# Head norm by tile inside a recurrence's levels, sample attention between window tiles, and the first output rows begun early

## The chip, the cores and the metric

The kernel runs on one core of one Trainium2 chip. The metric is the time of one execution in microseconds (us); the median of three runs is compared. The engines run side by side, each through its own queue of instructions in the order in which they are written, and they wait for one another on semaphores: TensorE (PE; its weight loads are PEld), VectorE (DVE), ScalarE (ACT), GpSimd (POOL), and SyncE (SP), which issues the transfers.

## The reference, cut to what matters

One decoder layer in fp32 for 512 prompt tokens and 8 sample tokens (520 columns in all). The part around the change is the hybrid mixer: a delta-rule recurrence over 8 heads of 64, with a norm over each head, a bonus and an output gate, beside a sliding-window attention; both halves go through one output projection.

```python
S_final, y = lax.scan(step, wkv0.astype(F32), seq)            # 8 heads x 64, state 64 x 64
y = jnp.moveaxis(y, 0, 1)
mu = jnp.mean(y, axis=-1, keepdims=True)
var = jnp.mean(jnp.square(y - mu), axis=-1, keepdims=True)
yn = ((y - mu) * lax.rsqrt(var + GN_EPS)).reshape(B, T, C)
yn = yn * lp['ln_x_w'].astype(F32) + lp['ln_x_b'].astype(F32)
out = (yn + bonus.reshape(B, T, C)) * g                        # g = sigmoid(xg) @ w_g_up
...
o = jnp.einsum('bnkgqs,bnskd->bnqkgd', pr.astype(v.dtype), vc) # window of 128, softmax with sinks
...
y = jnp.concatenate([y_rwkv, y_swa.astype(y_rwkv.dtype)], axis=-1) @ lp['w_out']
```

Cross attention over 256 memory tokens and a mixture of experts (32, two chosen for each token) follow. Neither is touched.

## The kernel before

The prompt's 512 tokens are four tiles of 128; the 8 sample tokens are a fifth, small tile. Activations lie transposed in SBUF, channels on partitions: `yT` has eight chunks of 128 channels by 520 tokens, chunks 0 to 3 from the recurrence and 4 to 7 from the windows. After the input projection comes the stage that matters here. One list, `RECUR_ORDER`, sets the order of its steps, and every engine walks the same list and does its own share of each step. Its names: `AB`, `N0`, `level` (six per tile, each doubling an inverse by 64x64 products for two groups of four heads, `XM`, `MM`, `NN`) and `fin` (`akv`, `G`, `WT`) prepare a tile of the recurrence; `U`, `S` and `Y` apply it in two half tiles, and `Y` writes the tile's outputs to `yT`. `rq`, `rk`, `vk` rotate queries and keys. `ws` is a tile's window scores with the first half of its softmax: TensorE multiplies into four banks, VectorE scales, masks and takes the maxima (L1990, L1963 to L1967), ScalarE exponentiates (`exps`, L1665, L1667). `wp` is the other half: VectorE normalises (`normalise`, L1979 to L1981), TensorE transposes the probabilities (`pT`), ScalarE copies them, TensorE multiplies them with the values (`o`), ScalarE copies that to `yT`.

All eight PSUM banks go round in the order of `bank_plan()`. A product waits until the bank's tenant eight places earlier has been copied out (`reuse`), the copying engine waits until the product is done (`filled`), and `done` is a wait for a copy.

When the list has ended, the kernel before does the rest in a row: `wkvT` and `ysT` transpose the last state and the samples' outputs; `mean`, `gate` and `var` are eight products each of 128x128 by 260 columns (head sums by the matrix `bones` of ones, and the gate's projection) over all four channel chunks and both halves of the columns; then VectorE divides chunk by chunk (`deviation_divided`, L2100 to L2103, the reciprocal over 128x520) and applies the gate (L2122), which raises `s_fin`. Among this, the samples' own window attention runs (`kT`, `qd`, `ss`, `ssT`, a softmax of one row per head, `spT`, `so`). The output projection (`output_share`) takes for each tile of tokens and each half of 512 columns four products of the window chunks and four of the recurrence chunks (128x128 by 512). Three of the window parts, (0, 0), (0, 1) and (1, 0), are done while `s_fin` is still awaited; the rest follows it. SP reloads x and loads w_out's two halves (`wo`) at the end of the stage.

## Time and profile before

| | |
|---|---|
| median of three runs | 836.73 us (835.77 to 839.98) |
| profiled execution, its own time | 839.23 us |
| its span in the profile | 837.4 us |
| mean granted clock of TensorE, of full speed | 0.894 |
| PE busy | 702.7 us, 84% |
| DVE busy | 371.4 us, 44% |
| ACT busy | 214.9 us, 26% |
| recurrence, from the first level to the last `WT` copied | 222.6 to 346.0 us |
| rest of the windows, norm, gate, samples, until `so` is copied | 346.0 to 444.5 us |
| rest of the output projection and its norms | 444.5 to 502.9 us |

Busy time is work in flight on an engine; a granted clock of 1.00 is TensorE's 2.4 GHz and 0.50 its 1.2 GHz. Times in the text are microseconds from the start of the span. An fp32 product of the program is two MATMUL instructions in the trace, a transpose is one; the order view below counts a product once.

### The profile page before, as it was taken

How to read it: one execution, taken by the hardware profiler on the slowest of the kernel's cores; microseconds unless marked ns; L12 is line 12 of the kernel's file. 1: busy time of each engine (PE TensorE's matmuls, PEld its weight loads, DVE VectorE, ACT ScalarE, POOL GpSimd, SP SyncE). 2: the span in 40 equal slices, each digit the busy share in tenths (PEclk: the TensorE clock that was granted, in tenths of full speed). 3: DMA queues.
4: the chain of work that ended last, by engine and by line, in shares of the span. 5: the costliest groups of instructions: out<-in, count | busy, mean ns of one | idle time of the engine just before them, and what ended most of it. 6: DMA issues, size and time to landing. Idle time of an engine off the chain costs nothing.

```text
span 837.4 us, 16076 instructions
## 1 busy us (share of the span) xinstructions
PE 702.7 (84%) x6956; PEld 530.7 (63%) x6956; DVE 371.4 (44%) x740; ACT 214.9 (26%) x538; POOL 92.4 (11%) x122
## 2 busy tenths in 40 slices
PE   3999999999979898667997989877699269999933
PEld 3874887878878888556753448655246257777711
DVE  4210129993365575645483330354325742222216
ACT  4250115334222222434501110322112002222214
POOL 0100000000765000000000000000000024344210
PEclk9999999999999999957988998975789569999966
DMA  9622340002101000320407011023608849999725
GB/s 309 245 101 100 101 139 13 1 1 59 61 4 54 3 4 4 114 47 2 180 28 270 31 56 45 1 79 96 209 25 327 354 144 377 409 405 405 307 93 237
DMA packets 42492, 113.90 MB, mean 136 GB/s; under 512 B 10187, under 2 KB 12677, under 8 KB 41116
## 3 DMA queue, kind: packets, MB, share of 16 engines
q1 hardware_dynamic: 36964, 102.18, 33.2%
q0 software_dynamic: 4864, 8.53, 2.9%
q10 hardware_dynamic: 592, 2.13, 0.7%
q8 instruction: 56, 0.92, 0.4%
q14 instruction: 16, 0.13, 0.0%
HBM read 105.88 MB, written 16.24 MB: 146 GB/s over the span
## 4 chain that ended last, share of the span: by engine, by line
PE 70%; DVE 18%; ACT 5%; issue 4%; DMA 2%; SPq 0%; POOL 0%; POOLq 0%; DVEq 0%; ACTq 0%
PE bank L874 51%; PE bank L1494 7%; PE bank L878 5%; PE bank L1508 4%; PE bank L1480 2%; DVE arena L1918 1%; PE bank L1502 1%; ACT arena L1667 1%; DMA arena<-pair_d 1%; DVE arena L2100 1%; DVE arena L1963 1%; DVE arena L2032 1%; ACT arena L1684 1%; DVE arena L1990 1%; DMA arena<-hn_d,arena 1%
## 5 line engine op out<-in xcount | busy, mean ns | idle before, releaser
L874 PE MATMUL bank<-arena 64*64 64x64 f32 (+11 forms) x5156 | 527.4, 296 | 60.2 <-DMA arena<-pair_d 11.8
L874 PEld LDWEIGHTS bank<-arena 64*64 64x64 f32 (+5 forms) x5156 | 392.4, 158 | 183.9 <-issue 102.7
L878 PE MATMUL bank<-arena 128*128 128x128 f32 (+4 forms) x392 | 58.2, 301 | 50.9 <-issue 16.6
L878 PEld LDWEIGHTS bank<-arena 128*128 128x128 f32 (+4 forms) x392 | 50.3, 167 | 66.1 <-issue 27.9
L1494 PEld LDWEIGHTS bank<-arena 128*64 128x64 f32 x1024 | 58.6, 138 | 19.7 <-issue 19.7
L830 POOL DMA_INDIRECT arena<-hn_d,arena x16 | 16.7, 1044 | 434.3 <-DVE arena L2299 412.1
L1494 PE MATMUL bank<-arena 128*64 128x128 f32 x1024 | 63.5, 276 | 0.0
L2320 DVE TENSOR_TENSOR arena<-bank,arena 128x512 f32<-128x512 f32 x32 | 22.1, 692 | 54.5 <-PE bank L1480 54.5
L1599 ACT COPY arena<-bank 128x260 f32<-128x260 f32 x40 | 15.0, 375 | 108.1 <-PE bank L874 108.1
L834 POOL DMA_INDIRECT pair_d<-arena x32 | 31.8, 993 | 61.1 <-ACT arena L1801 54.1
L1699 ACT COPY arena<-bank 128x256 f32<-128x256 f32 x56 | 20.8, 372 | 63.8 <-PE bank L874 62.3
L2142 DVE TENSOR_TENSOR arena<-arena,bank 128x512 f32<-128x512 f32 x16 | 10.9, 684 | 57.4 <-PE bank L874 57.4
L1508 PE MATMUL bank<-arena 128*64 128x512 f32 x128 | 35.4, 632 | 0.9 <-ACT arena L1797 0.9
L1738 ACT ACTIVATE arena<-arena 128x1024 f32<-128x1024 f32 (+1 forms) x10 | 10.6, 1057 | 94.8 <-DVE arena L2142 86.6
L1874 DVE COPY arena<-arena 128x9 f32<-128x9 f32 x14 | 2.4, 171 | 67.5 <-ACT arena L1599 67.2
L1801 ACT COPY arena<-bank 128x512 f32<-128x512 f32 x32 | 18.7, 585 | 46.2 <-PE bank L1508 46.2
L1480 PE MATMUL bank<-arena 128*128 128x128 f32 x128 | 23.7, 312 | 7.6 <-DMA arena<-hn_d,arena 7.6
L787 POOL TENSOR_TENSOR arena<-arena 128x256 f32<-128x256 f32 x8 | 5.0, 620 | 183.8 <-PE bank L874 183.8
L2331 DVE TENSOR_TENSOR arena<-arena,bank 128x64 f32<-128x64 f32 x32 | 7.1, 221 | 40.6 <-ACT arena L1795 40.6
L1480 PEld LDWEIGHTS bank<-arena 128*128 128x128 f32 x128 | 17.4, 197 | 10.1 <-issue 7.4
L2054 DVE TENSOR_TENSOR arena<-arena,bank 128x256 f32<-128x256 f32 x40 | 16.3, 419 | 11.9 <-PE bank L874 11.2
L2169 DVE TENSOR_REDUCE arena<-bank 128x2 f32<-128x512 f32 x8 | 5.5, 688 | 33.9 <-PE bank L874 33.8
(238 smaller groups left out, 550.2 us busy)
## 6 DMA issues: line engine op xcount, KB each, us to landing
arena<-in_w_exp_gate SPq DMA_DIRECT2D x32, 512.0 KB, 10.9
arena<-in_w_exp_up SPq DMA_DIRECT2D x32, 512.0 KB, 13.2
arena<-in_w_exp_down SPq DMA_DIRECT2D x32, 512.0 KB, 14.2
arena<-in_w_in SPq DMA_DIRECT2D x5, 2048.0 KB, 9.5
arena<-in_x_prompt SPq DMA_DIRECT2D x8, 512.0 KB, 6.2
arena<-in_w_out SPq DMA_DIRECT2D x2, 2048.0 KB, 10.9
arena<-in_cache_mem_k SPq DMA_DIRECT2D x8, 512.0 KB, 7.5
arena<-in_cache_mem_v SPq DMA_DIRECT2D x8, 512.0 KB, 3.8
```

The lines of the kernel that those rows point to most:

```text
L830: pool.indirect_dma_start(dst, None, hn_d, bass.IndirectOffsetOnAxis(rows.bitcast(U32), 0), bounds_check=NT - 1, oob_is_err=False).then_in ...
L834: pool.indirect_dma_start(half_rows, bass.IndirectOffsetOnAxis(rows.bitcast(U32), 0), src, None, bounds_check=2 * PAIRS_E - 1, oob_is_err= ...
L874: last[0] = pe.matmul(out, lhsT, rhs, start=start, stop=stop, skip_group_check=True)
L878: last[0] = pe.transpose(out, in_, ident[0:n, 0:n])
L1480: ins = pe.transpose(bX[(2 * p + i) % 3][:, k * P:(k + 1) * P], xk[:, 4 * i + k, :], ident)
L1494: ins = pe.matmul(o[BS * g:BS * g + BS, 0:2 * BS].rearrange("p (a f) -> p a f", a=2), rows[:, k, :], w[:, 0:2, lo:lo + BS], start=k == 0, ...
L1508: ins = pe.matmul(bY[b % 2][BS * n:BS * n + BS, :], actT, wdn[b % NW][:, n * 512:(n + 1) * 512], start=True, stop=True, skip_group_check=True)
L1599: return act.copy(dst, o[:, 0:HALF])
L1699: act.copy(dst[(n + 1) % 2][:, 4 * q:4 * q + 4, :], o[:, 0:256].rearrange("p (h t) -> p h t", h=4)).then_inc(evac["a"], 1)
L1801: act.copy(yb[b % NB3], bY[b % 2][:, :]).then_inc(s_ay, 1)
L2054: tt(Xi[:, qs, :], Xi[:, qs, :], o[:, 0:256].rearrange("p (h t) -> p h t", h=4), ALU.add) \
L2320: tt(xTe[p % 2][:, 4 * i:4 * i + 4, :], bX[n % 3][:, :].rearrange("p (k n) -> p k n", k=4), g, ALU.mult) \
```

## The change

The work that stood behind the list becomes steps of the list. `gate` products stand between the levels of tile 0. `mean`, `sq`, `var` of tile t-1 stand in tile t's levels: four products of 128x128 by 128 columns for the means, a Square on ScalarE, and four products with the squares as the stationary operand and two columns as the moving one, which give a variance per token and head (128x8) where before it was spread over all channels (4 x 128x520). `rstd` takes the root on ScalarE and the reciprocal on VectorE of that small array, once for tiles 0 to 2 and once for tiles 3 and 4 (`GROUPS`). `rb` spreads it back over the channels by products with the identity, and `y_final` multiplies, adds the bonus and applies the gate, again once per group. `wp` is split into `wt` (normalise, transposes) and `wv` (values). The steps of the windows and of the samples come in another order, and `wo` projects tile 0's output rows (sixteen products) before the last window tile and the samples' attention are done. Loads of x for tiles 2 to 4 wait for the norm, since the gate now lies in their place.

The core of the diff:

```diff
+RECUR_ORDER = [("AB", 0, 0), ("AB", 0, 1), ("N0", 0, 0),
+               ("level", 0, 0), ("gate", 0, 0), ("level", 0, 1), ("gate", 0, 1),
...
+        RECUR_ORDER += [("level", _t, 2), ("rq", 2 * _t - 2, 0), ("mean", _t - 1, 0), ("level", _t, 3),
+                        ("rq", 2 * _t - 2, 1), ("sq", _t - 1, 0), ("level", _t, 4), ("rq", 2 * _t - 1, 0),
+                        ("level", _t, 5), ("var", _t - 1, 0), ("rq", 2 * _t - 1, 1)]
...
         RECUR_ORDER += [("rk", 0, 0), ("level", _t, 2), ("rk", 0, 1), ("rk", 1, 0), ("level", _t, 3), ("rk", 1, 1),
-                        ("vk", 0, 0), ("level", _t, 4), ("ws", 0, 0), ("level", _t, 5)]
+                        ("vk", 0, 0), ("mean", 2, 0), ("level", _t, 4), ("ws", 0, 0), ("sq", 2, 0), ("level", _t, 5),
+                        ("var", 2, 0)]
     RECUR_ORDER += [("fin", _t, 0)]
-RECUR_ORDER += [("ws", 1, 0), ("U", 3, 0), ("wp", 0, 0), ("S", 3, 0), ("ws", 2, 0), ("U", 3, 1), ("wp", 1, 0),
-                ("S", 3, 1), ("ws", 3, 0), ("Y", 3, 0), ("wp", 2, 0), ("wp", 3, 0)]
+RECUR_ORDER += [("rstd", 0, 0), ("U", 3, 0), ("wt", 0, 0), ("S", 3, 0), ("wv", 0, 0), ("U", 3, 1), ("ws", 1, 0),
+                ("Y", 3, 0), ("S", 3, 1), ("wkvT", 0, 0), ("ysT", 0, 0), ("ws", 2, 0), ("wt", 1, 0),
+                ("mean", 3, 0), ("mean", 4, 0), ("wv", 1, 0), ("ws", 3, 0), ("kT", 0, 0), ("sq", 3, 0), ("sq", 4, 0),
+                ("wt", 2, 0), ("var", 3, 0), ("var", 4, 0), ("ss", 0, 0), ("wv", 2, 0), ("rb", 0, 0), ("ssT", 0, 0),
+                ("rstd", 1, 0), ("wo", 0, 0), ("wt", 3, 0), ("wv", 3, 0), ("rb", 1, 0), ("spT", 0, 0), ("so", 0, 0)]
+GROUPS = ((0, 3), (3, 5))
...
+            def head_variances(t, _):
+                R = tile_rows(t)
+                pe.wait_ge(s_ysq, t + 1)
+                o = reuse(pe, ("var", t))
+                for c in range(4):
+                    src = ysq[:, c, :] if t < TILES else ysqS[:, c, :]
+                    mm(o[0:R, 2 * c:2 * c + 2], src, bones[:, 0:P:HD])
+                close()
+
+            def deviations_spread(g, _):
+                pe.wait_ge(s_rs, g + 1)
...
+                            for e in range(2):
+                                mm(o[64 * e:64 * e + 64, n:n + R],
+                                   rs[0:R, t, 2 * c + e:2 * c + e + 1].to_broadcast([R, HD]), ident[0:R, 0:R])
...
+            def first_rows_projected(t, _):
+                weights_in(pe, ("wo", 1))
+                done(pe, ("o", t))
+                for n in range(2):
+                    output_share(t, n, windows, True)
+                    if n == 0:
+                        weights_in(pe, ("wo", 0))
+                        pe.wait_ge(s_fin, 1)
+                    output_share(t, n, recurrence, False)
+                    close()
...
+                elif what == "sq":
+                    R = tile_rows(t)
+                    done(act, ("mean", t))
+                    act.activation(ysq if t < TILES else ysqS, yT[:, 0:4, t * P:t * P + R], ACT.Square) \
+                        .then_inc(s_ysq, 1)
...
+                elif what == "rstd":
+                    lo, hi = GROUPS[t]
+                    done(act, ("var", hi - 1))
+                    act.activation(rs[:, lo:hi, :], rs[:, lo:hi, :], ACT.Sqrt, scale=1.0 / HD,
+                                   bias=small[:, 40:41]).then_inc(s_dev, 1)
...
+            def y_final(g):
+                lo, hi = GROUPS[g][0] * P, min(GROUPS[g][1] * P, NT)
...
+                    ins = stt(yT[:, c, lo:hi], o[:, n:n + W], pcol("ln_x_w", c), yT[:, c, lo:hi], ALU.mult, ALU.mult)
...
+                    ins = stt(yT[:, c, lo:hi], yT[:, c, lo:hi], pcol("ln_x_b", c), PR[:, 8 + c, 1 + lo:1 + hi],
+                              ALU.add, ALU.add)
+                link(ins)
+                done(dve, ("gate", 3, 1))
+                tt(yT[:, 0:4, lo:hi], yT[:, 0:4, lo:hi], gateS[:, :, lo:hi], ALU.mult).then_inc(s_fin, 1)
...
-                link(dve.reciprocal(ydev[:, c, :], ydev[:, c, :]))
```

Where it moves instructions, first on TensorE at the end of tile 3's levels. In the program before: level 4 (32 products), the scores of window tile 0 (128x128 x8), then level 5, `akv`, `G` and `WT` (64x64 x64) in one run.

```order
L874 MATMUL bank<-arena 64x64 x32
L874 MATMUL bank<-arena 128x128 x8
L874 MATMUL bank<-arena 64x64 x64
L874 MATMUL bank<-arena 128x256 x8
L874 MATMUL bank<-arena 64x64 x8
L878 MATMUL bank<-arena 128x128 x8
L874 MATMUL bank<-arena 64x128 x8
```

In the changed program, at the same place: the mean of tile 2 (128x128 x4), level 4, the scores, level 5 (64x64 x16), the variances of tile 2 (128x2 x4), then `akv`, `G`, `WT` and the first `U` (56).

```order
L898 MATMUL bank<-arena 128x128 x4
L898 MATMUL bank<-arena 64x64 x32
L898 MATMUL bank<-arena 128x128 x8
L898 MATMUL bank<-arena 64x64 x16
L898 MATMUL bank<-arena 128x2 x4
L898 MATMUL bank<-arena 64x64 x56
L902 MATMUL bank<-arena 128x128 x8
```

Four variance products now stand ahead of `akv`, and the scores of window tile 1 (128x256 x8), which followed `WT`, have moved behind the transposes of tile 0 (L902).

ScalarE at the same place, changed program: the eight exponentials of window tile 0 (L1733), then tile 2's Square (L1788), the copy of its variances (L1793), `WT`'s copies (L1771), the root (L1797) with its table load, and the copies of tile 0's transposed probabilities (L1750).

```order
L1731 ACTIVATE arena<-arena 128x8
L1733 ACTIVATE arena<-arena 128x128 x8
L1788 ACTIVATE arena<-arena 128x512
L1793 COPY arena<-bank 128x8
L1771 COPY arena<-bank 128x4x64 x2
L1797 ACT_TABLE_LOAD
L1797 ACTIVATE arena<-arena 128x24
L1750 COPY arena<-bank 128x2x128 x4
```

The Square, its copy and the root stand between the exponentials and the copies; before, `WT`'s copies came straight after the exponentials.

VectorE towards the end, changed program: `y_final` of tiles 0 to 2 (L2078, L2083, L2087), the samples' scores and maxima (L2207 to L2043), the second reciprocal, the residual adds of tile 0 (L2223), and only then the normalisation of window tile 3 (L2055 to L2057) and `y_final` of tile 3 and the samples.

```order
L2078 SCALAR_TENSOR_TENSOR arena<-bank,arena 128x384 x4
L2083 SCALAR_TENSOR_TENSOR arena<-arena 128x384 x4
L2087 TENSOR_TENSOR arena<-arena 128x4x384
L2207 TENSOR_SCALAR arena<-bank 64x128
L2039 TENSOR_REDUCE arena<-arena 64x1
L2041 TENSOR_TENSOR arena<-arena 64x1
L2042 TENSOR_TENSOR arena<-arena 64x1
L2043 TENSOR_SCALAR arena<-arena 64x1
L2191 RECIPROCAL arena<-arena 128x16
L2223 TENSOR_TENSOR arena<-arena,bank 128x512 x2
L2055 TENSOR_TENSOR arena<-arena 128x8
L2056 RECIPROCAL arena<-arena 128x8
```

The normalisation of window tile 3 stood ahead of the whole norm before; now it stands behind the projection of the first rows.

## Rows read from the trace of the kernel before

**Rows 1.** The page: the span, and each engine's busy time, share and instructions.
```profile
span 837.4 us, 16076 instructions
...
PE 702.7 (84%) x6956; PEld 530.7 (63%) x6956; DVE 371.4 (44%) x740; ACT 214.9 (26%) x538; POOL 92.4 (11%) x122
```
**Rows 2.** Timeline of PE in the levels: start us, us, engine line, count, [idle before].
```profile
222.58 14.70 PE L874 MATMUL bank<-arena 64*64 64x64 f32 x480 [2.00 <-DVE arena L2038]
...
249.04 22.27 PE L874 MATMUL bank<-arena 64*64 64x64 f32 x618 [2.58 <-DVE arena L2038]
```
**Rows 3.** Busy time of DVE in a stretch of tile 1's levels 3 to 5.
```profile
262.30:272.40 10.10, 8.78 (x21) 1.00 0.27 108
```
**Rows 4.** Timeline of PE from tile 3's level 4 to the windows' end.
```profile
335.82 5.73 PE L874 MATMUL bank<-arena 64*64 64x64 f32 x144
343.28 5.12 PE L874 MATMUL bank<-arena 64*64 64x64 f32 x96 [1.73 <-DVE arena L2063]
354.45 1.94 PE L878 MATMUL bank<-arena 128*128 128x128 f32 x8 [6.04 <-issue]
357.09 10.50 PE L874 MATMUL bank<-arena 128*64 128x128 f32 x80 [0.70 <-ACT arena L1684]
374.19 3.65 PE L878 MATMUL bank<-arena 128*128 128x128 f32 x16 [6.60 <-issue]
378.52 10.52 PE L874 MATMUL bank<-arena 128*64 128x128 f32 x178 [0.68 <-ACT arena L1684]
...
397.24 2.04 PE L874 MATMUL bank<-arena 128*64 128x128 f32 x32 [0.68 <-ACT arena L1684]
```
**Rows 5.** Timeline of ACT: the last exponential of window tile 0, then `WT`'s copies.
```profile
345.25 0.19 ACT L1667 ACTIVATION_READ_ACCUMULATOR arena<-arena 128x1 f32 x1
345.34 0.62 ACT L1704 COPY arena<-bank 128x256 f32<-128x256 f32 x2
```
**Rows 6.** Timeline of DVE: window tile 2's last bank, its maxima, tile 1's normalisation.
```profile
366.58 0.69 DVE L1990 SCALAR_TENSOR_TENSOR arena<-bank,arena 128x512 f32<-128x512 f32 x1 [0.59 <-PE bank L874]
367.31 2.29 DVE L1963 TENSOR_REDUCE arena<-arena 128x8 f32<-128x2048 f32 x1
...
371.36 0.17 DVE L1979 TENSOR_TENSOR arena<-arena 128x8 f32<-128x8 f32 x1
371.56 0.20 DVE L1980 RECIPROCAL arena<-arena 128x8 f32<-128x8 f32 x1
371.80 2.29 DVE L1981 TENSOR_TENSOR arena<-arena 128x2048 f32<-128x2048 f32 x1
```
**Rows 7.** Clock by stretch: busy PE, PEld, DVE, ACT, POOL, then PEclk, DMA share, GB/s.
```profile
352.00:382.50 30.50, 20.07 (x142) 16.97 (x144) 11.88 (x20) 12.43 (x43) 0.00 (x0) 0.50 0.20 43
...
420.25:427.00 6.75, 6.75 (x19) 4.31 (x18) 5.98 (x7) 0.00 (x0) 0.00 (x0) 0.50 0.02 8
```
**Rows 8.** Timeline of PE from `mean` to the output projection.
```profile
405.23 11.26 PE L874 MATMUL bank<-arena 128*128 128x260 f32 x52 [0.28 <-DVE arena L2084]
...
418.31 10.24 PE L874 MATMUL bank<-arena 64*128 64x4 f32 x40 [0.95 <-ACT arena L1730]
...
436.55 3.69 PE L874 MATMUL bank<-arena 128*64 128x2 f32 x64 [0.32 <-DVE arena L2118]
444.58 18.87 PE L874 MATMUL bank<-arena 128*128 128x512 f32 x40 [4.34 <-DVE arena L2125]
...
464.18 13.90 PE L874 MATMUL bank<-arena 128*128 128x512 f32 x32
```
**Rows 9.** Groups of DVE from 395 to 500 us: count, busy us, mean ns.
```profile
L2100 DVE RECIPROCAL arena<-arena 128x520 f32<-128x520 f32 x4 | 13.6, 3396 | 2.0 <-ACT arena L1726 2.0
...
L2090 DVE SCALAR_TENSOR_TENSOR arena<-bank,arena 128x260 f32<-128x260 f32 x8 | 3.1, 422 | 0.8 <-PE bank L874 0.8
```
**Rows 10.** Timeline of ACT at the first root: table load and next instruction.
```profile
412.95 1.28 ACT L1726 ACT_TABLE_LOAD   x1
414.25 3.05 ACT L1726 ACTIVATE arena<-bank,arena 128x260 f32<-128x260 f32 x8
```

More of the change, by code:

```diff
@@ L671, in _, with load_projection @@
                     .then_inc(s_cache, 16)
+            def load_projection(i):
+                key, s, src, k = loads[i]
+                sp.dma_start(weights(key, k), src).then_inc(s_w[s], 16)
+            sp.wait_ge(full, place[("Y", 3, 1)] + 1)
+            load_projection(n_early + 1)
+            sp.dma_start(x[:, 0, :], A["x_prompt"][0, 0:P, :]).then_inc(s_xr[0], 16)
+            sp.dma_start(x[:, 1, :], A["x_prompt"][0, P:2 * P, :]).then_inc(s_xr[1], 16)
             done(sp, ("wkvT",))
@@ L1214, in window_outputs @@
                 close()
-            steps = {"rq": rotated_query, "rk": rotated_key, "vk": window_values, "ws": window_scores,
-                     "wp": window_outputs, "sample": lambda *_: None,
-                     "tok": by_token, "AB": chunk_products, "N0": first_N, "level": level, "fin": last_products,
-                     "U": updates, "S": state, "Y": outputs}
-            for what, t, n in RECUR_ORDER:
-                steps[what](t, n)
-            o = reuse(pe, ("wkvT",))
-            done(pe, ("S", 3, 1))
@@ new lines, in states_turned, with sample_outputs_turned @@
+            def states_turned(*_):
+                o = reuse(pe, ("wkvT",))
+                done(pe, ("S", 3, 1))
+                for c in range(4):
+                    tr(o[0:64, c * P:(c + 1) * P], ST[:, 8, c, :])
+                close()
+            def sample_outputs_turned(*_):
+                pe.wait_ge(s_ysl, 16)
+                o = reuse(pe, ("ysT",))
+                for c in range(4):
+                    tr(o[:, c * NS:(c + 1) * NS], ysr[:, c * P:(c + 1) * P])
+                close()
@@ L1313, in _ @@
+            for what, t, n in RECUR_ORDER:
+                steps[what](t, n)
+            done(pe, ("o", 3))
             done(pe, ("so",))
-            pe.wait_ge(s_fin, 1)
-            weights_in(pe, ("wo", 0))
+            pe.wait_ge(s_fin, 2)
             def rows_transposed(key, first, t):
@@ L2138, in residual @@
                     ins.then_inc(evac["v"], 1)
-                for n in range(2 if t < TILES else 0):
+                for n in range(2 if t < TILES and not begun else 0):
                     o = filled(dve, (key, t, n))
```

345 lines of the change are left out of this document (186 added, 159 removed).

## The prediction

> **What bounds the kernel now.** I read the page first, then the clock by stretch, then each engine's timeline between 220 and 503 us. TensorE is busy for 84% of the span [rows 1], so the first question for moved work is whether TensorE has room where it lands. In the levels of the recurrence it has none: tile 0's run of 480 instructions takes 14.70 us and tile 1's run of 618 takes 22.27 us without an idle gap inside [rows 2]. The reader is to see there that a product added between levels is paid in full. VectorE has 1.3 us free in 10.1 us of tile 1's levels 3 to 5 [rows 3], so it has no more room than TensorE at that place.
>
> After the levels, from 346 to 404 us, the stage is bound by the round trip of the window softmax, not by one engine. TensorE stands idle for 6.04 and 6.60 us ahead of the transposes at 354.45 and 374.19 [rows 4]. The trace puts these waits down to "issue"; the programs' order and rows 6 say what they are: after the last bank of window tile 2 (366.58) VectorE takes 0.69 us, then 2.29 us and the small steps for the maxima, and only then tile 1's normalisation (0.17, 0.20, 2.29 us), which ends at 374.09. The transposes start 0.1 us later. In this stretch the granted clock is 0.50, the lower level (1.2 GHz), from 352 to 382.5 us [rows 7]; it fell after an idle gap, so that the gap costs twice.
>
> From 415 to 444.5 us VectorE sets the end: four reciprocals over 128x520 take 13.6 us [rows 9], and TensorE waits for the last of that work for 4.34 us [rows 8]. This is the wait that the change removes.
>
> **The change part by part.** The profiled execution has a span of 837.4 us and a time of 839.23 us; the median of the runs is 836.73 us, 2.5 below it. I sum on the span and add the difference to the median.
>
> *Products from the tail into the levels.* The 26 products at 405.23 (8 means, 8 gates, 8 variances, 2 small) take 11.26 us [rows 8], 0.433 us each. Eight gates in tile 0 cost 8 x 0.433 = 3.5 us, since TensorE has no gap there [rows 2]. A mean of one tile is four products of 128 columns: 4 x 0.433 x 128/260 = 0.85 us. For a variance of two columns there is no such row: `so` has 64 instructions with two columns in 3.69 us [rows 8], 0.058 each, so eight instructions are 0.46 us; the weights here are twice as wide, so up to 0.9; I take 0.6. VectorE's subtraction of the mean (128x512, 0.69 us [rows 6]) fits beside the mean's product, the variance lies half under VectorE's backlog. I take 1.35 us for each of tiles 1 and 2 (bounds 0.85 and 2.1): 2.7 us. **Levels: +6.2.** From here on I keep the axis of the trace before and leave these 6.2 out.
>
> *The wait at tile 3.* Here the moved work does more than fill time. The variances of tile 2 need its Square, and the Square stands on ScalarE behind the eight exponentials of window tile 0 (both orders are shown above). Those end at 345.44 [rows 5]; with tile 2's mean (+0.85) at 346.25; a Square over 128x512 is about 0.6 us (ScalarE's two copies of 256 columns take 0.62 [rows 5]), so TensorE gets to the variances at 346.9. It has done level 5 by 341.5: level 4, scores, level 5 and `akv` are the 5.73 us from 335.82 [rows 4], less `akv`'s 0.9 (32 instructions at 14.70/480 [rows 2]), plus 0.85. It then stands for 5.4 us, and behind the wait are `akv`, `G` and `WT`, so also VectorE's copies and `U`. From the variances: 1.0, `akv` 1.9 (32 instructions at the lower level, which I expect after such a gap), copy 0.7, `G` 1.9, `WT` about 1.5, ScalarE's copies 0.62 [rows 5]: 353.5. Before, `WT` was copied at 345.96. **Wait: +7.5** (bounds 6.0 at full clock, and 9).
>
> *From `WT` to the samples' end.* The path before takes 345.96 to 444.53 us, 98.6. The new one, step by step. ScalarE loads a table (1.28 [rows 10]) and takes the root, VectorE inverts 128x24 and does `U`'s three small adds (1.2): 356.5. It normalises window tile 0, half as wide as tile 1, in about 1.6: 358.1. TensorE transposes (1.94) and then has the same 80 instructions as before at 357.09 (10.50 [rows 4]), with tile 1's scores in place of tile 2's: 370.6. `Y` and the second `S` are 130 instructions of the 178 that took 10.52; 6.2, so 376.8; the state's copy and two small transposes 1.2; the scores of tile 2 3.4 (eight products of 256 columns at 0.426): 381.4. Now the same round trip: last bank and maxima 3.6, normalisation 2.75 [rows 6]: 387.8, and TensorE has stood for 6.4 us. Transposes of tile 1 at the lower clock 3.65 [rows 4], means 1.25, values 2.04 [rows 4], scores of tile 3 3.4, `kT` 1.2: 399.4. Round trip again: 405.0, idle 5.6. Transposes 3.65, variances 1.4, `ss` 3.4 (32 of the 40 instructions at 418.31 [rows 8], most of them at 0.50 [rows 7]), values 2.7, `rb` of 48 instructions at 2.04/32 each 3.1 [rows 4]: 419.3. `y_final` on VectorE: at 0.42 for 260 columns [rows 9] and 0.69 for 512 [rows 6], 384 columns take 0.55; last bank 0.55, four adds 2.2, gate over 1536 columns 1.75 (2.29 for 2048): 423.9. The window half of the first rows (four products of 13.90/16 = 0.87 us [rows 8]) lies under that, the other twelve take 10.4: 434.4. Only then does VectorE reach tile 3's normalisation: add 0.7, 2.75: 437.8, idle 3.4. Transposes 2.4, values 2.4, `rb` 1.8, `y_final` of 136 columns behind it 2.2: 446.6. Samples' normalisation, transpose and copy 1.3, `so` 3.69 [rows 8] to 5 at the lower clock, copy 0.2: 452.3. That is 98.8 us from `WT`. **Tail: +0.2.** VectorE's 13.6 us of reciprocals and the 11.26 us of products are gone, but 13.9 us of projection and about 5 us of `rb` stand in their place, and the scores of each window tile come one round later.
>
> *The rest.* At 444.58 twenty products were left of the first two tiles, 18.87 us [rows 8]. Now sixteen are left: 13.9, and 1.0 for the lower clock after `so`. **Rest: -4.0.** What follows is the same program. w_out's and x's loads move, but they are issued over 15 us ahead of their use.
>
> Sum: 6.2 + 7.5 + 0.2 - 4.0 = 9.9 us, so a span of 847.3 and a median of 836.73 + 9.9 = 846.6 us.
>
> *What the skill says here.* Each switch of the root's and the exponential's tables costs 1.30 us in this trace, load and all: the load starts at 412.95 and the next instruction at 414.25 [rows 10]. The Trainium skill, ScalarE: Activation LUTs, What ACT_TABLE_LOAD costs, puts a switch at 1283 ns for the load and about 1380 ns more for a drain. By the page the first root would come 1.4 us later and the sum, as an estimate, would be 11.3. The trace has the load but no drain in front of the next instruction, so I stay with the row.
>
> **The rivals.**
>
> *The moved products are free.* If the levels have gaps which the timeline merges away, the 6.2 us of step one cost nothing: 840.4 us, no change that can be told. For it: TensorE's ends are modelled. Against it: tile 1's run is paced evenly and VectorE is as full [rows 2, 3].
>
> *The clock stays up.* The tail has more for TensorE between softmax rounds. If the granted clock were 1.00 from `WT` on, the same steps end earlier: `WT` at 352.0, window tile 1's scores at 363.8, tile 2's at 372.1, tile 1's normalisation at 378.4, tile 2's at 394.5, `rb` at 405.9, `y_final` at 410.4, first rows at 420.9, `so` at 438.0. That is 14.3 us less than 452.3: 9.9 - 14.3 = -4.4, a time of 832.3 us, faster. It decides between `WT` and the end of `Y`, where I have 17 us of half clock. Against it: before, the clock stayed at 0.50 from 352 to 382.5 us though TensorE was busy for 20.07 of 30.5 us [rows 7], and I count gaps of 5.4, 4, 6.4 and 5.6 us, as long as those that it fell in.
>
> *VectorE's end is all that counts.* One could take the 29 us from 415.1 to 444.5, put 9 us of `y_final` against 24 us of division and gate, and forecast 822 us. Against it: `y_final` waits for `rb`, and `rb` for window tile 2 ahead of it on TensorE, which the sum shows to be as late as before.
>
> *The lower clock also in the first rows.* Twelve more products at half speed and a slower `so` are up to 7 us: 854 us.
>
> **How the numbers follow.** The sum's own case, 842 to 853, has 0.58 (the wait's bounds, and 4 us either way for the clock of the tail). Free products: 0.17. Clock up: 0.15. VectorE alone: 0.03. Lower clock in the first rows: 0.07. About 0.5% (4.2 us) is what a measurement of this kernel can tell from no change. So faster 0.18, same 0.17, slower 0.65. The range goes from 834 to 854, which leaves out most of the clock's rival and the last one's end; the likeliest case's own range is 842 to 853. The time is the likeliest's, 846.6 us.
>
> **What would show it.** In the changed profile: TensorE's run in tile 0's levels is about 3.5 us longer; an idle gap of about 5 us ahead of the variances at tile 3, released by the Square on ScalarE; `WT` copied about 13.7 us later than before (7.5 + 6.2); three gaps of 5 to 6.5 us ahead of the windows' transposes, and one of about 3.4 us ahead of tile 3's; a clock of 0.50 through window tile 1's scores; `so` copied near 458 us; VectorE's busy time about 17 us lower. The prediction is wrong if the clock is 1.00 after `WT`, or if the Square does not come late; then the time falls towards 832 to 840.

## The result, and the profile after

The changed kernel takes 848.65 us (median of four runs, 846.91 to 858.77), the kernel before on the same chip 838.13 (four runs): ratio 1.014 [1.010, 1.0185]: slower by 1.4%, with an interval clear of 1. A second comparison gave 854.38 against 837.5, ratio 1.0215 [1.0176, 1.0253]. The profiled execution is the shortest of the first four: 846.91, with a span of 845.1 against 837.4 before. So the profiles differ by 7.7 us where the medians differ by 10.5; the terms below add up to the 7.7.

The page of the changed kernel, answering to [rows 1]:

```profile
span 845.1 us, 16345 instructions
...
PE 710.4 (84%) x7084; PEld 539.8 (64%) x7084; DVE 356.1 (42%) x734; ACT 216.1 (26%) x542; POOL 92.4 (11%) x122
```

VectorE has lost 15.3 us of work (371.4 to 356.1), and the kernel is slower, so the time went elsewhere. Timeline of TensorE in the levels of tiles 0 and 1, answering to [rows 2]:

```profile
223.54 20.95 PE L898 MATMUL bank<-arena 64*64 64x64 f32 x496 [2.00 <-DVE arena L2134]
...
256.24 16.18 PE L898 MATMUL bank<-arena 64*64 64x64 f32 x494 [2.58 <-DVE arena L2134]
```

Tile 0's levels take 20.95 us instead of 14.70. The levels start 0.96 us later (in a second profile 0.9 earlier, so this is chance). From one tile's start to the next: tile 0 32.70 us (before 26.46), tile 1 33.73 (33.41), tile 2 33.44 (33.41). Then timeline of TensorE from tile 3's level 4 to the first rows' product, answering to [rows 4] and [rows 8]:

```profile
343.26 5.79 PE L898 MATMUL bank<-arena 128*128 128x128 f32 x120
354.43 3.77 PE L898 MATMUL bank<-arena 128*128 128x2 f32 x40 [5.39 <-ACT arena L1788]
358.99 2.83 PE L898 MATMUL bank<-arena 64*64 64x64 f32 x64 [0.79 <-DVE arena L2159]
...
367.23 1.97 PE L902 MATMUL bank<-arena 128*128 128x128 f32 x8 [3.54 <-DVE arena L2057]
369.13 11.35 PE L898 MATMUL bank<-arena 64*64 64x64 f32 x210
...
392.90 3.68 PE L902 MATMUL bank<-arena 128*128 128x128 f32 x16 [6.34 <-DVE arena L2057]
...
410.52 3.68 PE L902 MATMUL bank<-arena 128*128 128x128 f32 x16 [5.37 <-DVE arena L2057]
413.98 12.70 PE L898 MATMUL bank<-arena 128*128 128x2 f32 x128
...
431.48 10.54 PE L898 MATMUL bank<-arena 128*128 128x512 f32 x24 [1.12 <-issue]
445.44 3.60 PE L902 MATMUL bank<-arena 128*128 128x128 f32 x16 [3.42 <-DVE arena L2057]
449.77 4.18 PE L898 MATMUL bank<-arena 128*64 128x128 f32 x64 [0.72 <-ACT arena L1750]
457.22 0.36 PE L902 MATMUL bank<-arena 64*128 64x64 f32 x1 [3.27 <-DVE arena L2057]
457.90 6.58 PE L898 MATMUL bank<-arena 128*64 128x2 f32 x64 [0.32 <-DVE arena L2213]
464.81 16.28 PE L898 MATMUL bank<-arena 128*128 128x512 f32 x32 [0.33 <-issue]
```

The reader sees one wait on ScalarE (L1788, the Square) and five on a normalisation (L2057). Timeline of ScalarE at the first of them, answering to [rows 5] and [rows 10]:

```profile
353.67 0.19 ACT L1733 ACTIVATION_READ_ACCUMULATOR arena<-arena 128x1 f32 x1
353.76 0.62 ACT L1788 ACTIVATE arena<-arena 128x512 f32<-128x512 f32 x1
356.33 0.17 ACT L1793 COPY arena<-bank 128x8 f32<-128x8 f32 x1 [1.95 <-PE bank L898]
361.87 0.65 ACT L1771 COPY arena<-bank 128x256 f32<-128x256 f32 x2 [5.37 <-PE bank L898]
362.54 1.28 ACT L1797 ACT_TABLE_LOAD   x1
363.83 0.31 ACT L1797 ACTIVATE arena<-arena 128x24 f32<-128x24 f32 x1
```

`WT` is copied at 362.52 (345.96 before). The clock in stretches of the changed kernel, the columns as in [rows 7]:

```profile
224.00:227.50 3.50, 3.50 (x62) 3.24 (x58) 0.55 (x2) 1.45 (x4) 2.19 (x4) 0.55 0.49 162
353.50:374.00 20.50, 14.48 (x193) 13.03 (x193) 5.05 (x11) 5.72 (x14) 0.00 (x0) 0.50 0.26 52
374.00:388.00 14.00, 10.52 (x172) 8.48 (x170) 10.00 (x17) 6.20 (x21) 0.00 (x0) 0.98 0.53 196
388.00:398.00 10.00, 5.10 (x26) 5.10 (x26) 4.68 (x7) 6.39 (x21) 0.00 (x0) 0.51 0.74 267
...
415.00:418.50 3.50, 3.50 (x41) 3.46 (x41) 0.19 (x1) 0.71 (x3) 0.00 (x0) 0.97 0.02 5
418.50:425.50 7.00, 7.00 (x66) 6.98 (x68) 0.89 (x3) 0.59 (x1) 0.00 (x0) 0.53 0.00 0
446.00:449.00 3.00, 3.00 (x15) 2.64 (x13) 0.00 (x0) 1.76 (x3) 0.00 (x0) 0.50 0.00 0
456.00:469.50 13.50, 11.64 (x71) 8.81 (x72) 2.34 (x8) 0.00 (x0) 0.00 (x0) 0.50 0.51 163
```

With 408 to 415, where it is 0.51 too, the lower level (1.2 GHz) holds for 61 us of 353.5 to 469.5.

The span falls into these stretches (us; "query" and "expert product" are the first products of the cross attention and of the experts):

| stretch | before | after | difference | predicted |
|---|---|---|---|---|
| ahead of the levels | | | +1.0 | 0 |
| tile 0's to tile 3's levels | 93.3 | 99.9 | +6.6 | +6.2 |
| tile 3's levels to `WT` copied | 30.1 | 39.1 | +9.0 | +7.5 |
| `WT` to `so` copied | 98.6 | 102.2 | +3.6 | +0.2 |
| `so` to the first query product | 58.4 | 55.8 | -2.6 | -4.0 |
| cross attention, to the first expert product | 177.0 | 170.3 | -6.7 | 0 |
| experts, to the end | 157.5 | 154.3 | -3.2 | 0 |
| span | 837.4 | 845.1 | +7.7 | +9.9 |

From tile 0's levels to the first query product the changed part lost 16.6 us (6.6 + 9.0 + 3.6 - 2.6), not 9.9, and the untouched program behind it came out 9.9 shorter.

### The profile page after: what moved, and what is told of

It reads as the page before. It is cut to its first block, busy times and chain, and to the rows that moved or that the text cites. A ratio compares the mean times of both kernels' runs of the same rounds, so it can differ in the third digit from the quotient of the medians.

```text
span 845.1 us, 16345 instructions
## 1 busy us (share of the span) xinstructions
PE 710.4 (84%) x7084; PEld 539.8 (64%) x7084; DVE 356.1 (42%) x734; ACT 216.1 (26%) x542; POOL 92.4 (11%) x122
## 4 chain that ended last, share of the span: by engine, by line
PE 72%; DVE 18%; ACT 3%; issue 3%; DMA 3%; SPq 0%; DVEq 0%; POOLq 0%
PE bank L898 52%; PE bank L1560 7%; PE bank L902 6%; PE bank L1574 4%; PE bank L1546 3%; DVE arena L2057 1%; DVE arena L1994 1%; DVE arena L2039 1%; PE bank L1568 1%; ACT arena L1733 1%; DMA arena<-in_norm_mix 1%; DMA arena<-pair_d 1%; DVE arena L2066 1%; DVE arena L2128 1%; DVE arena L2457 1%
## 5 line engine op out<-in xcount | busy, mean ns | idle before, releaser
L898 PE MATMUL bank<-arena 64*64 64x64 f32 (+11 forms) x5284 | 535.5, 295 | 59.8 <-DMA arena<-pair_d 11.7
L898 PEld LDWEIGHTS bank<-arena 64*64 64x64 f32 (+5 forms) x5284 | 401.1, 159 | 183.2 <-issue 104.2
L902 PE MATMUL bank<-arena 128*128 128x128 f32 (+4 forms) x392 | 60.4, 308 | 52.2 <-DVE arena L2057 31.9
L902 PEld LDWEIGHTS bank<-arena 128*128 128x128 f32 (+4 forms) x392 | 51.9, 171 | 66.7 <-DVE arena L2057 36.7
L2150 DVE TENSOR_TENSOR arena<-arena,bank 128x256 f32<-128x256 f32 x40 | 16.2, 418 | 16.6 <-PE bank L898 16.1
```

The lines of the kernel that those rows point to most:

```text
L898: last[0] = pe.matmul(out, lhsT, rhs, start=start, stop=stop, skip_group_check=True)
L902: last[0] = pe.transpose(out, in_, ident[0:n, 0:n])
L2150: tt(Xi[:, qs, :], Xi[:, qs, :], o[:, 0:256].rearrange("p (h t) -> p h t", h=4), ALU.add) \
```

## The experiments

The experiments are called by their numbers, e1 to e11. e1 to e4 ran beside the kernel before at 838.33 us; e5, e6, e8 and the repeat of the changed kernel on the same chip beside 837.5; e7, e9, e10 and e11 on another chip beside 835.5. Ratios are to the kernel before of the same group. Places ("`so` at") are read from one profiled execution of each kernel, ratios from all its runs.

**e1: the Square ahead of window tile 0's scores.** Edit to the changed kernel:

```diff
-("mean", 2, 0), ("level", _t, 4), ("ws", 0, 0), ("sq", 2, 0), ("level", _t, 5),
+("mean", 2, 0), ("level", _t, 4), ("sq", 2, 0), ("ws", 0, 0), ("level", _t, 5),
```

> The changed kernel with tile 2's Square moved ahead of window tile 0's exponentials on ScalarE; nothing else. Theory (the Square behind the exponentials holds TensorE back before the variances, and akv, G, WT with it): the 5.39 us gap of TensorE before the variances at tile 3 goes, WT is copied 6 to 9 us earlier (near 354 us instead of 362.5), and the time falls by 4 to 8 us against the changed kernel, to about 841 to 844. Rival (the wait is hidden by the softmax round trip behind it): WT is copied earlier, but the transposes of window tile 1 still start near 392.9 us, and the time stays within 1.5 us of 847.

Measured: 848.91 us, 1.0106 [1.0069, 1.0143]. The profiled execution is the longest of its six (span 856.5). Its TensorE timeline and the clock behind it:

```profile
352.69 1.61 PE L898 MATMUL bank<-arena 64*64 64x64 f32 x64 [0.79 <-DVE arena L2159]
355.28 0.68 PE L898 MATMUL bank<-arena 64*64 64x64 f32 x16 [0.98 <-ACT arena L1771]
359.95 1.97 PE L902 MATMUL bank<-arena 128*128 128x128 f32 x8 [3.98 <-DVE arena L2057]
...
358.00:399.00 41.00, 32.04 (x274) 27.43 (x274) 18.23 (x30) 15.00 (x47) 0.00 (x0) 0.50 0.42 144
```

The wait of 5.39 us is gone and `WT` is copied at 355.23, 8.0 us earlier counted from tile 3's start: the cause of the wait is the Square's place. But the clock, which in the changed kernel was back at 374, stayed at 0.50 for 41 us, and `so` came at 468.95, 4.2 us later than in the changed kernel (464.71). That it is the longest execution doesn't explain this: e5, below, has the same 41 us. The time was forecast at 841 to 844 and missed that. The ratio stands 0.4 to 1.1% below the changed kernel's two (1.014 and 1.0215), 3 to 9 us for the 8.0; its interval overlaps that of the first of them.

**e2: the gates out of tile 0's levels.** The eight gate products go ahead of tile 0's and tile 1's levels, where TensorE has gaps.

```diff
-("level", 0, 0), ("gate", 0, 0), ("level", 0, 1), ("gate", 0, 1), ...
+("gate", 0, 0), ("gate", 0, 1), ("gate", 1, 0), ("gate", 1, 1)] + [("level", 0, k) for k in range(6)] + ...
+        [("gate", c, n) for c in (2, 3) for n in range(2) if _t == 1] + [("level", _t, 0), ...
```

> The changed kernel with the eight gate products taken out from between tile 0's levels: four stand after tile 0's N0, where TensorE waited 2.00 us for VectorE, and four after tile 1's N0, where it waited 2.58 us. Theory (between levels they are paid in full, 6.25 us in the profile, 3.5 by their own durations and the rest by the clock and by switching): tile 0's run of levels is back at 14.7 us, the gaps take most of the products, and the first level of tile 3 starts 3 to 6 us earlier, time about 842 to 845. Rival (moved products cost the same wherever they stand): the start of tile 3's levels moves by under 1 us.

Measured: 852.11 us, 1.0168 [1.0133, 1.0202]. Tile 1's levels start at 251.88 instead of 256.24; of these 4.4 us about 1.3 are the changed kernel's fall of the clock at 224, which e2 doesn't have. A fall of the clock at 286 to 289.5, which the changed kernel doesn't have, then makes tile 2 take 34.99 us instead of 33.44, so that tile 3's start is 2.8 us earlier (3 to 6 expected) and `so` 2.7. The ratio lies between the changed kernel's two: so small a gain can't be told.

**e3: window tile 3's transposes ahead of the first group's norm.**

```diff
-("wv", 2, 0), ("rb", 0, 0), ("ssT", 0, 0), ("rstd", 1, 0), ("wo", 0, 0), ("wt", 3, 0), ("wv", 3, 0), ("rb", 1, 0),
+("wv", 2, 0), ("wt", 3, 0), ("rb", 0, 0), ("wv", 3, 0), ("ssT", 0, 0), ("rstd", 1, 0), ("wo", 0, 0), ("rb", 1, 0),
```

> The changed kernel with the normalisation and transposes of window tile 3 ahead of the spread deviations (rb) and its values product behind them, so that they no longer wait for tile 0's output rows. Theory (the projection of the first rows in front of the last window tile makes a new wait): the gap of 3.42 us before those transposes and the 0.72 after them go, so is copied 3 to 5 us earlier than at 464.5, time about 843 to 845. Rival (VectorE's end is moved by the same amount, so nothing is won): so is copied within 1 us of 464.5.

Measured: 846.11 us, 1.0094 [1.0064, 1.0123]. The gap of 3.42 us is gone, `so` comes at 457.94, 6.8 us earlier and so more than the 3 to 5 expected; the cross attention then takes 174.9 us instead of 170.3 in this profile, with 14.7 us more of half clock in it. The ratio is 0.5 to 1.2% below the changed kernel's two; its interval just overlaps that of the first.

**e4: extra products in the waits.** Products of 128x128 by 512 columns whose result is overwritten, in six waits of the stage: ahead of the transposes of the four window tiles (below), 5 ahead of tile 2's variances and 3 ahead of the samples' transposed weights. The output is the same.

```diff
+                o = reuse(pe, ("pT", t, 0))
+                for _ in range((3, 6, 5, 3)[t]):
+                    mm(o[:, :], ident, maskAB.rearrange("p a t -> p (a t)"))
                 pe.wait_ge(s_prob, t + 1)
```

> The changed kernel with extra products of constants (128x128 by 512 columns, results overwritten) in TensorE's waits: 3, 6, 5, 3 ahead of the transposes of window tiles 0 to 3, 5 ahead of tile 2's variances, 3 ahead of the samples' transposed weights. They add no result and are meant to be shorter than the waits at the full clock. Theory (the gaps lower the clock, and half clock costs about 10 us of the stage from 354 to 470 us): the granted clock stays at 1.00 through most of that stretch, so is copied 8 to 14 us earlier than at 464.5, time about 835 to 840. Rival (the round trips of VectorE and ScalarE set the pace and TensorE's clock only changes how long it waits): the clock is up, but so moves by under 3 us.

Measured: 842.63 us, 1.0049 [1.0030, 1.0068]. The changed kernel's clock between 353.5 and 374 and from there to 460, then the same two stretches with the extra products:

```profile
353.50:374.00 20.50, 14.48 (x193) 13.03 (x193) 5.05 (x11) 5.72 (x14) 0.00 (x0) 0.50 0.26 52
374.00:460.00 86.00, 63.39 (x542) 50.48 (x541) 39.50 (x73) 28.33 (x84) 0.00 (x0) 0.82 0.20 72
```

```profile
353.50:374.00 20.50, 16.83 (x290) 13.44 (x292) 9.20 (x18) 6.29 (x14) 0.00 (x0) 0.92 0.24 53
374.00:460.00 86.00, 76.93 (x541) 52.94 (x536) 36.40 (x70) 26.71 (x83) 0.00 (x0) 0.90 0.25 90
```

Work that computes nothing makes the kernel faster (0.9 to 1.6% below the changed kernel's two ratios, the intervals apart), if not as fast as the 835 to 840 us expected; `so` comes 9.7 us earlier. The lower level remains in 357.5 to 360.5, 408.5 to 418.5 (10.00 us busy of 10.00; it begins in `ss`, products of 4 columns) and 453 to 459.5 (`so`).

**e5: all three orders at once**, the edits of the first three experiments together.

> The changed kernel with the three edits together: Square ahead of the exponentials, gates in the waits after N0, last window tile ahead of the spread deviations. Theory (each edit takes away a wait or a price of its own): 8.0 us for WT, 4.4 for the start of tile 1 and 6.8 for so, as measured one by one, add up to so copied 14 to 19 us earlier than at 464.7 if the clock comes as in the changed kernel's profile, time 834 to 841. Rival (the clock takes back what an earlier WT gives, as the profile of the Square alone showed): so is copied 8 to 12 us earlier, time 841 to 845.

Measured: 838.76 us, 1.0026 [0.9996, 1.0055]: no longer to be told from the kernel before. Against the changed kernel beside it (854.38) that is 15.6 us, near the 8.0, 2.7 and 6.8 of the single edits; by the first ratio, 1.014, it is 1.2%, about 10 us. In its profile (842.7, one of the longer executions) `so` is only 9.7 us earlier, as the rival had it, so the theory held by the time and the rival by the place. `WT` is copied at 350.76, `so` at 455.06, with the clock at 0.50 in 353.5 to 394.5, 404.5 to 421.5 and 445.5 to 459.5.

**e6: the window tiles in their old order**, on top of e5.

```diff
-RECUR_ORDER += [("rstd", 0, 0), ("U", 3, 0), ("wt", 0, 0), ("S", 3, 0), ("wv", 0, 0), ("U", 3, 1), ("ws", 1, 0), ...
+RECUR_ORDER += [("ws", 1, 0), ("rstd", 0, 0), ("U", 3, 0), ("wt", 0, 0), ("ws", 2, 0), ("S", 3, 0), ("wv", 0, 0), ...
```

> The three edits, and the window tiles one round earlier: scores of tile 1 before U and the root, of tile 2 straight after tile 0's transposes, of tile 3 straight after tile 1's. Theory (the tail's length is the softmax round trips, and the change put each tile's scores one round later): so is copied another 5 to 10 us earlier than with the three edits, time 828 to 836, at or below the kernel before. Rival (VectorE's own work per window tile, 8.2 us, sets the pace once the rounds are closer): under 3 us.

Measured: 842.56 us, 1.0070 [1.0045, 1.0095]. TensorE's waits of over 2.9 us in window tiles 0 and 1:

```profile
363.79 1.97 PE L901 MATMUL bank<-arena 128*128 128x128 f32 x8 [12.23 <-DVE arena L2056]
...
386.83 3.68 PE L901 MATMUL bank<-arena 128*128 128x128 f32 x16 [3.15 <-DVE arena L2056]
```

The rival, a gain of under 3 us, held: `so` comes at 456.42, 1.4 us later than in e5. Against e5 tile 1's wait shrinks from 6.35 to 3.15 (and tile 2's from 5.37 to 2.92), and tile 0's grows from 3.98 to 12.23, since VectorE does tile 1's scores ahead of tile 0's normalisation. For tiles 0 and 1 together 10.33 us have become 15.38.

**e8: extra products in the kernel before**, in the waits ahead of `pT` and of `s_fin`.

```diff
+                for _ in range((5, 6, 3, 0)[t]):
+                    mm(o[:, :], ident, maskAB.rearrange("p a t -> p (a t)"))
                 pe.wait_ge(s_prob, t + 1)
...
+            for _ in range(4):
+                mm(o[:, :], ident, maskAB.rearrange("p a t -> p (a t)"))
             pe.wait_ge(s_fin, 1)
```

> The kernel before with extra products of constants in TensorE's waits: 5, 6, 3 ahead of the transposes of window tiles 0, 1, 2 and 4 ahead of the wait for s_fin; no result is added. Theory (the lower clock from 352 to 382.5 us, and again at 393, 420 and 441, costs the kernel before about as much as it costs the changed one): clock 1.00 through most of 352 to 420 us, so copied 6 to 12 us earlier than at 444.5, time 827 to 833. Rival (the round trips set the pace): under 3 us.

Measured: 833.46 us, 0.9916 [0.9878, 0.9954]. Its TensorE timeline at window tile 0's transposes, which stood at 354.45 before, and from the samples' end:

```profile
357.22 1.09 PE L878 MATMUL bank<-arena 128*128 128x128 f32 x8 [1.51 <-DVE arena L1987]
...
437.40 12.88 PE L874 MATMUL bank<-arena 128*64 128x2 f32 x81 [0.32 <-DVE arena L2124]
```

The time is 0.8% shorter, but the profile doesn't show it where I expected it. `so` comes at 445.38, 0.9 us later than before (444.52), not 6 to 12 earlier. Ahead of any extra product its clock falls at 223, 250, 284 and 318, in place of two falls before, and the levels are 1.3 us longer up to tile 3's start and another 1.5 up to these transposes. From tile 0's transposes to `so` it takes 88.2 us instead of 90.1: 1.9 us, though the half clock between 352 and `so` has fallen from 45 to 27 us. By the place the rival, under 3 us, held: in this profile the lower clock of the stage had cost the kernel before little. Where its runs gain the 0.8% is not shown; the profiled one (835.73) is among the longer of ten.

**The changed kernel again** (after_again): 

> The changed kernel unaltered, for a second profile and for times beside these runs on the same chip. Theory (the order of the work makes the loss, the clock's ups and downs in cross attention differ from run to run): the marks up to so agree with the first profile within 2 us, from so on the lengths differ by up to 7 us. Rival: all lengths agree within 1 us, so that the 9 us given back after the stage belong to the change.

Measured: 854.38 us, 1.0215 [1.0176, 1.0253]; `WT` 360.81, `so` 463.09, queries 518.94, experts 690.39, span 844.5: all stretches of the table but the first (-0.9 for +1.0) are reproduced within 1.2 us, so by the places the rival nearly held. But both profiles are of the shortest execution of their group (846.91 and 846.41). The other five of this group took 853.02 to 860.44, at a mean clock of 0.877 to 0.890 instead of 0.896, and none of them was profiled: where the median of 854.38 loses another 8 us is not shown.

**e7: three orders and extra products**: e5 with the loops of e4, (3, 6, 5, 0) ahead of `pT` and 3 ahead of `spT`.

> e5_three_orders with the extra products of e4_fill_waits (their results are overwritten, the output is the same) in the waits ahead of the transposes of tiles 0, 1 and 2 (3, 6, 5 of 128x512) and of the samples' (3). Theory: e5 gained 11 us of work until `WT` is copied and lost most of it to a granted clock of 0.50 from 353.5 to 394.5, 404.5 to 421.5 and 445.5 to 459.5. With the waits filled, `so` is copied 8 to 12 us earlier than its 455.06, that is at 443 to 447, and the time is 829 to 834 us, ratio 0.990 to 0.995. Rival: the softmax's round trips on VectorE bound this stage whatever the clock; then `so` is within 3 us of 455 and the time 836 to 840.

Measured: 826.68 us, 0.9871 [0.9825, 0.9916]. Clock by stretch:

```profile
351.89:401.50 49.61, 43.31 (x438) 31.98 (x438) 27.55 (x48) 24.53 (x78) 0.00 (x0) 1.00 0.40 131
401.50:408.50 7.00, 7.00 (x50) 6.65 (x50) 2.75 (x4) 1.46 (x3) 0.00 (x0) 0.51 0.00 0
436.00:442.50 6.50, 6.17 (x35) 4.56 (x35) 1.03 (x3) 0.00 (x0) 0.00 (x0) 0.50 0.40 136
```

`so` comes at 439.37, 15.7 us before e5's, more than the 12 that I had as the upper bound; the half-clock time in the stage falls from 72 us to 13.5. e9, below, has the same program up to there, and its profile has 34 us of half clock and `so` at 441.94: a place read from one profile is known to about 3 us. The extra products are worth 1.5% on top of the orders (1.0026 to 0.9871), about as much as the orders are on top of the changed kernel (1.2 to 1.9%).

**e9: the same in the cross attention.** e7, and the same loop ahead of the waits for the prompt tiles' probabilities, the samples' scores and the samples' probabilities.

```diff
+                for _ in range((0, 1, 3, 0)[t]):
+                    mm(o[:, :], ident, maskAB.rearrange("p a t -> p (a t)"))
                 pe.wait_ge(s_prob, 6 + t)
```

> e7_orders_and_fills, and extra products of 128x512 in the waits of the cross attention too: 1 and 3 ahead of the transposes of prompt tiles 1 and 2, 3 ahead of the samples' scores' transposes, 6 ahead of the samples' probabilities' (L2279 and L2057 release these waits in the changed kernel, 2.77 and 6.20 us). This asks whether the cross attention's length, 170.3 us in the changed kernel and 177.0 before, is set by the clock. Theory: yes; from the first query product to the first expert product it takes 166 to 171 us, and the clock is 1.00 for all but a few us of it; the time is 1 to 5 us below e7's. Rival: the length follows from something else (VectorE's pace, the caches' loads); then it stays 171 to 178 and the time is e7's.

Measured: 818.19 us, 0.9746 [0.9693, 0.9800], the fastest kernel of all, 8.5 us below e7 where I had 1 to 5. From query to expert products it takes 164.6 us, less than the 166 to 171 expected, and this with the clock at the lower level for 51.5 us of it, not "a few". The kernel before and this one at the third prompt tile's transposes and the samples' two waits:

```profile
568.73 1.97 PE L878 MATMUL bank<-arena 128*128 128x128 f32 x8 [5.03 <-DVE arena L1981]
...
589.99 0.58 PE L878 MATMUL bank<-arena 128*32 128x128 f32 x2 [2.77 <-DVE arena L2182]
...
604.85 0.42 PE L878 MATMUL bank<-arena 32*128 32x32 f32 x2 [5.50 <-DVE arena L1981]
```

```profile
561.55 1.09 PE L901 MATMUL bank<-arena 128*128 128x128 f32 x8 [2.46 <-DVE arena L2068]
...
577.79 0.38 PE L901 MATMUL bank<-arena 128*32 128x128 f32 x2
...
591.62 0.31 PE L901 MATMUL bank<-arena 32*128 32x32 f32 x2 [1.43 <-DVE arena L2068]
```

**e10: the kernel before with both**: e8, and e9's loops with (0, 1, 5, 0), 3 and 5.

> The kernel before with e8's extra products in the stage and those of the cross attention (1 and 5 ahead of the transposes of prompt tiles 1 and 2, 3 and 5 for the samples'). Theory of the clock: cross attention 177.0 in the kernel before, 175.6 in e8; here 167 to 172, and a time 4 to 8 us below e8's ratio of 0.992, that is a ratio of 0.983 to 0.988. Rival: it stays at 0.990 to 0.993, the length of 175 being VectorE's.

Measured: 824.93 us, 0.9846 [0.9795, 0.9897]; cross attention 164.6 us. Both kernels come to the same 164.6 there, and since e10 differs from e8 (175.6) and e9 from e7 (174.8) only by what fills these waits, the waits and the clock behind them make this difference. Over all fourteen profiles it goes roughly with the time at the lower clock in it: 51.5 and 52 us give 164.6 (e9, e10); 74.5 to 79.3 us give 170.2 to 171.5 (e2, the changed kernel twice, e4, e6), but once 174.8 (e7); 84.8 to 92.4 us give 174.9 to 177.7 (before, e8, e3, e1, e11, e5). `so` is at 447.21, no earlier than before, so the gain of this kernel lies behind the stage. With the waits filled on both sides, the change in its new orders is 0.8 to 1% faster than the kernel before (818.19 and 824.93 us; 0.9746 and 0.9846, whose intervals just touch).

**e11: narrow extra products**: e4, with each loop longer (14, 30, 26, 14 ahead of the transposes, 26 and 14 in the other two waits) and its product two columns wide.

```diff
+                    mm(o[:, 0:2], ident, maskAB[:, 0, 0:2])
```

> The changed kernel with extra products in the same five waits as e4_fill_waits, but each of 128x128 by 2 columns instead of 512 (14, 30, 26, 14, 26 and 14 of them), about as long in time. It asks what in e4 helped: that TensorE's queue was not empty, or that its array multiplied. If products of 2 columns hold the clock as those of 512 did, the clock is 1.00 for nearly all of 353 to 460 and the ratio is 1.003 to 1.007, as e4's 1.0049. If they do not, the clock is 0.50 in the stage for 50 us or more, as in the changed kernel (61 us from 353.5 to 469.5), and the ratio is 1.012 to 1.022, as the changed kernel's. I expect the second, 0.7: the samples' `so` (64 instructions of two columns) ran at 0.50 in both kernels.

Measured: 872.31 us, 1.0431 [1.0384, 1.0478], far above both. I had sized them wrongly: the group of these products in 392 to 404.6, and the clock there:

```profile
L898 PE MATMUL bank<-arena 128*128 128x2 f32 x60 | 11.5, 329 | 0.0
```

```profile
392.00:395.00 3.00, 2.86 (x20) 2.47 (x20) 1.83 (x3) 0.83 (x3) 0.00 (x0) 0.97 1.02 416
395.00:404.50 9.50, 9.50 (x46) 9.50 (x47) 4.39 (x7) 4.25 (x17) 0.00 (x0) 0.50 0.74 269
```

Thirty of them (60 instructions) take 11.5 us in a wait of 6.3, so the time tells nothing of the clock. The clock does: it falls at 395, 2.7 us into a run without a gap whose last 2 us are these products, and stays at 0.50 through the rest of them, 9.50 us busy of 9.50. 75 us of 354 to 484 are at the lower level. So an occupied TensorE was not enough to keep the clock; in this stage products of 512 columns did and products of two did not.

## Why the prediction was wrong where it was

The time was 2.0 us from the forecast and the sign was right, but by luck in part: the changed stage lost 6.7 us more than the sum had, and the untouched program came out 9.9 shorter. `so`, which I had near 458, was copied at 464.71. The second comparison's 854.38 lies 7.8 us off.

**Products into the levels** (+6.2 predicted, +6.6 measured). The gates in tile 0 were mis-sized: 6.2 us for 3.5. In part this is a fall of the clock at 224 to 227.5 that the kernel before had later, at 250 to 253 and 284 to 287.5. e8, the kernel before with an early fall (223 to 226.5), has 27.79 us for tile 0 against 26.46, so such a fall costs 1.3, and the gates 4.9: 0.61 each among the 64x64 products, not the 0.433 of a run of like products. The groups of TensorE in the changed kernel's tile 0 have the same 4.9 of busy time, though part of it at the lower clock:

```profile
L898 PE MATMUL bank<-arena 128*128 128x260 f32 x16 | 4.9, 416 | 0.0
```

Tiles 1 and 2 show +0.3 and 0.0 where I had 1.35 each; they no longer have the two falls, and with 1.3 added for each the means and variances come to 1.6 and 1.3, as forecast. The rival of free products is excluded: e2 gained 4.4 us by tile 1 through taking the gates out of tile 0, about 3 of them without the clock's part.

**The wait at tile 3** (+7.5, measured +9.0, the upper bound). The mechanism is exact: an idle 5.39 us for 5.4, ended by the Square, which took the 0.62 that was taken for it, and e1 removes it. What was short is the work behind it: from the variances to `WT` copied it took 8.1 us where I had 6.6 (346.9 to 353.5). The items that I listed add up to 7.6, so 1.0 of the 1.5 is a slip in adding; the variances and `akv` took 3.77 for 2.9, `G` and `WT` 2.83 for 3.4 (e1, at full clock, has 1.61).

**`WT` to `so`** (+0.2, measured +3.6). The gaps came as listed: 3.54, 6.34, 5.37, 3.42 for 4, 6.4, 5.6, 3.4. VectorE's steps came as listed too: root to normalised tile 0 in 4.65 us for 4.6, `rb` to the gate's end in 4.75 for 4.6, twelve projections in 10.54 for 10.4. The step that failed is where I put the half clock: through window tile 1's scores and then little of it. It was back at 374, so the scores of tile 2 ended 3.9 us earlier than in my sum, and up to `so` it fell five times more (at 387.5, 408, 418.5, 445.5 and 456), where the sum had half clock only at tile 1's and tile 2's transposes, in `ss` and in part of `so`. From the transposes of tile 1 each step is compared with its own length in the sum: tile 1's transposes to `kT` took 0.7 more, window tile 2's transposes to the end of `rb` 1.9 more (half clock in 418.5 to 425.5), tile 3's transposes to the samples' normalisation 3.0 more (half clock in 446 to 449, and a wait of 3.27 that I had as 2.2 of `y_final`), the samples' end with `so` (6.58 for the 5 at most) 1.8 more. These add up to 7.4; less the 3.9 that is +3.5.

**The rest** (-4.0, measured -2.6). The first sixteen products took 16.28 us, since the clock was at 0.50 until 469.5: 2.4 more than 13.9, for the 1.0 that I had.

**"What follows is the same program"** is the step that failed most: -9.9 in place of 0. The same instructions took 170.3 us instead of 177.0 in the cross attention, and across the profiles 170.2 to 177.7. e9 and e10 show what it hangs on: with the waits filled both kernels take 164.6. The sum had to name this as open and give it a width: the second profile of the changed kernel has 171.5, but e1 and e3, the same program there, 175.0 and 174.9. What decides where the clock falls in it, and so why this kernel's was shorter than before, was not tested. Why the experts took 3.2 us less stays open; e1 to e11 have 154.0 to 156.7 there.

**The rivals.** "The clock stays up" gave 14.3 us less for the stage's tail. It didn't happen, but its price was about right: e4, with a clock mostly at 1.00, has `so` 9.7 us earlier. "VectorE's end is all that counts" is excluded: VectorE stands idle for 6.11 us ahead of the residual add behind which tile 3's normalisation stands, and 7.45 ahead of the last `y_final`, both times for TensorE. "The lower clock in the first rows" half happened, in the rows after `so`. The reason given for the low clock, gaps of 4 to 6 us, is borne out by e4 against the changed kernel and e7 against e5, which differ in nothing but what fills these gaps. But "the gap costs twice", which I read from the profile before, holds for the changed kernel only: there filling gives 9.7 us up to `so`, in the kernel before 1.9 (e8). The Trainium skill, TensorE: Matmul & The Clock Gate, A second HAM failure mode: psum-queue depth-cycling, tells of a kernel whose short idle times between groups make the clock go back and forth, at a cost of throughput. This case agrees, with 61 us of 116 at the lower level. What made the clock return at 374 in the changed kernel but only at 399 in e1 was not settled.

So in its profile the change loses by a wait that it made and the half clock behind it (9.0), by gates put where TensorE was full (about 4.9, and 1.3 for the fall of the clock among them) and by half clock and a late last window tile up to `so` (3.6), against 2.6 us less to project at the end and 9.9 behind the stage whose cause is open. That its orders are to blame is shown by e5, whose ratio of 1.0026 can't be told from 1. VectorE's 15.3 us less work bought nothing here: the stage ends by the softmax's round trips and TensorE's products between them.

## What to carry to other kernels

Where TensorE stands idle for some microseconds again and again, ask for each gap what the work behind it costs at half clock, and test it by filling the gap with wide products, not narrow ones: against the kernel before that gave 0.8% with the stage's waits filled, 1.5% with the cross attention's too, and 2.5% together with the change in better orders. Look afterwards where the time went: in e8 the clock was up and the stage hardly shorter. Judge an order of steps by repeated times: in single profiles a gain of 7 or 8 us at one place was taken back at the next by a fall of the clock, wholly in e1 and in part in e3. Before a step is moved between others on a queue, look on every engine that it uses for what it lands behind: here eight exponentials ahead of one Square cost 9 us, of which the wait itself is 5.4.

## What the runs showed that I had not expected

- The clock falls under work without a gap: in the changed kernel at 418.5, after 3.50 us busy of 3.50 with products of 2 and 4 columns, and it stays low for 7.00 busy of 7.00, nearly all of it products of 128 columns; in e11 it stays at 0.50 through 9.50 busy of 9.50 of products of two columns.
- An fp32 product of two columns with weights 128 wide is dear. In e11 16 of its instructions take 2.1 us at full clock (0.13 each) and 46 take 9.9 at half (0.22); `so`, with weights 64 wide, takes 0.058 and 0.103. From the 0.058 I had 0.6 us for the eight of a tile's variances; e4 has them in 1.0 at full clock.
- The same cross attention takes 170.2 to 177.7 us in kernels that differ only ahead of it, and 164.6 with its waits filled.
- The same kernel has executions of 846 and of 853 to 860 us on one chip; a profile of the first tells nothing of what the others lose.
